# Differential attention: the first batch of a unit's transposes is copied out by ScalarE, in front of its exponentials

## The chip, the core and the metric

The kernel runs on one core of a Trainium2 chip. Its engines are TensorE (PE in the profile, PEld for its weight loads), VectorE (DVE), ScalarE (ACT), GpSimd (POOL) and SyncE (SP, which issues DMAs). Each works through its own list of instructions in order, and waits on semaphores for the others. The time is that of the device from start to end of one execution, in microseconds (us).

## The reference

A trunk of two layers on 2048 tokens of width 1024. Each layer projects the tokens once, runs three groups of attention heads on the result (latent, differential, windowed), gates and concatenates them, projects the result and normalises. The change is in the differential group: 4 heads, each with two softmax maps of which the second is subtracted, scaled by a learned factor.

```python
def block(args):                       # one block of 128 queries
    qb, bi = args
    ...
    sc = jnp.einsum('bqhmd,bkhmd->bmhqk', qb, k).astype(jnp.float32) * scale + bias[None, None]
    p = jax.nn.softmax(sc, axis=-1)
    a = p[:, 0] - lam * p[:, 1]
    return jnp.einsum('bhqk,bkhd->bqhd', a.astype(v.dtype), v)
```

## The kernel before

A layer runs in five stages: input projection, latent attention, differential attention, window attention, output projection. Between stages all engines meet at a barrier.

The function `diff_attention` works in *units*. A unit `n` is one head and one block of 128 queries, so there are 64 in a layer (4 heads of 16 blocks). Per unit there are four *score pairs*, `scores(n, m, half)`: map `m` (0 or 1) and half of the 2048 keys, each two matmuls of 128x512 into two PSUM banks. Where the band of the position bias (the block of keys at the query block and its neighbours) falls into that half, further matmuls (line 1480) add it: in the lower half of the keys for the first blocks of a head, in the upper half for the last. Three such pairs of banks form a ring, so score pair `i` of the count over all units waits until the exponential of pair `i - 3` is done.

The steps of a unit, by engine:

- TensorE: `scores` (lines 1474, 1480), `turns(n, c)` (line 1492), which transposes a quarter of the mixed probabilities, four 128x128 blocks, into the one bank TURN, and `products` (line 1507), which multiplies the transposed probabilities of two units with the values.
- VectorE: `maximum` (line 1613) of each score pair, `to_shift` (line 1620), which makes the exponential's bias of the two maxima of a map, `ratios` (lines 1629 to 1636), copies out of TURN (line 1647) and `output` (line 1656).
- ScalarE: `exp` (line 1545), two exponentials of 128x1024 for a map, `scale` (line 1552) for a quarter of the second map, copies out of TURN (line 1562) and `odd_half` (line 1570), once in two units.
- GpSimd: the rest of the mixing of the two maps, `p0 + ratio * p1`: lines 1593, 1597, 1599 and 1602. Line 1593 waits for the ratio, and line 1597 for ScalarE's `scale`.

There is one bank TURN. Batch `c` of the transposes can be made only when the copy of the batch before it is done. All copies count up the semaphore `copied`, whichever engine makes them; TensorE and the copiers take the batches in the same order.

The work is skewed by hand. Each of the three engines has one loop over `n`, and the order of the calls in its body is the order of its instructions. In round `n` the scores are those of unit `n`, and the transposes are those of unit `n - LAG` with `LAG = 2`, the last batch (and on VectorE the third) one round later. TensorE's round is: scores(n, 0, 0), batch 3 of unit n-3, scores(n, 0, 1), products, batch 0 of unit n-2, scores(n, 1, 0), batch 1, scores(n, 1, 1), products, batch 2. Batches 0 and 2 were copied by VectorE, batches 1 and 3 by ScalarE.

Of the kernel before, what the change touches and what calls it, by code (L numbers as in the profile page):

```python
# [1367 lines left out]
def diff_attention(shared, layer, carry, split_d, v_d, band_d, side_d, block_d, o_d, totals):  # L1368
# [10 lines left out]
    LAG = 2  # L1379
# [4 lines left out]
    with ctx:  # L1384
# [24 lines left out]
        def banks(n, m, half):  # L1409
            slot = (4 * n + 2 * m + half) % SLOTS  # L1410
            return psum[:, 2 * slot:2 * slot + 2, :]

        with nc.Block() as block:
# [115 lines left out]
            def copy_args(n, c):  # L1529
                dst = turned[:, n // 2 % 2, 4 * c:4 * c + 4, n % 2 * P:(n % 2 + 1) * P]  # L1530
                return dst, psum[:, TURN, :].rearrange("p (k n) -> p k n", n=P)

            @block.scalar
            def _(act):
                def exp(n, m):
                    act.wait_ge(shifted, 2 * n + m + 1)
                    if m == 0 and n >= DEEP:
                        act.wait_ge(turn_done, 4 * (n - DEEP + 1))
                    if m == 1 and n >= DEEP1:
                        act.wait_ge(mixed, 2 * (n - DEEP1 + 1))  # L1540
                    dst = probs[:, n % DEEP, :] if m == 0 else probs1[:, n % DEEP1, :]
                    if m == 0 and n >= 2:
                        act.wait_ge(summed, n - 1)
                    for half in range(2):
                        nc.scalar.activation(dst[:, half * HALF:(half + 1) * HALF].rearrange("p (a n) -> p a n", n=CH),  # L1545
                                             banks(n, m, half), ACT.Exp, bias=shift[:, n % 2, m:m + 1], scale=DIFF_SCALE,
                                             accum_out=row_sum[:, n % 2, m, half:half + 1]).then_inc(exped, 1)

                def scale(n):
                    act.wait_ge(ratio_ready, n + 1)  # L1550
                    first = probs1[:, n % DEEP1, 0:CH]
                    nc.scalar.activation(first, first, ACT.Copy, scale=ratio[:, n % 2:n % 2 + 1]).then_inc(act_scaled, 1)  # L1552

                def copy(n, c):
                    if not 0 <= n < UNITS:
                        return
                    act.wait_ge(turn_done, 4 * n + c + 1)
                    if n >= 4:

                        act.wait_ge(pv_done, n // 2 - 1)  # L1560
                    dst, src = copy_args(n, c)
                    nc.scalar.activation(dst, src, ACT.Copy).then_inc(copied, 1)

                def odd_half(g):
                    if not 0 <= g < GROUPS:
                        return
                    act.wait_ge(pv_done, g + 1)
                    if g >= 2:
                        act.wait_ge(o_ready, g - 1)
                    nc.scalar.activation(odd[:, g % 2, :], psum[DV:P, PV, 0:2 * P], ACT.Copy).then_inc(odd_out, 1)  # L1570

                act.wait_ge(dots_ready, 1)
                nc.scalar.activation(dots[:, 2:4], dots[:, 0:2], ACT.Exp).then_inc(dots_exp, 1)
                for n in range(UNITS + DRAIN + 2):
                    on = n < UNITS
                    copy(n - LAG - 1, 3)
                    if on:
                        exp(n, 0)
                    copy(n - LAG, 1)
                    if 1 <= n <= UNITS:  # L1580
                        scale(n - 1)
                    if n % 2:
                        odd_half((n - 5) // 2)
                    if on:
                        exp(n, 1)
# [24 lines left out]
            def _(dve):  # L1610
                def maximum(n, m, half):
                    dve.wait_ge(scored, 4 * n + 2 * m + half + 1)
                    nc.vector.tensor_reduce(row_max[:, n % 2, m, half:half + 1], banks(n, m, half), AX.XY, ALU.max  # L1613
                                            ).then_inc(maxed, 1)

                def to_shift(n, m):
                    dve.wait_ge(maxed, 4 * n + 2 * m + 2)
                    if n >= 2:
                        dve.wait_ge(exped, 4 * (n - 2) + 2 * m + 2)
                    nc.vector.tensor_scalar(shift[:, n % 2, m:m + 1], row_max[:, n % 2, m, 0:1],  # L1620
                                            row_max[:, n % 2, m, 1:2], -DIFF_SCALE, ALU.max, ALU.mult
                                            ).then_inc(shifted, 1)

                def ratios(n):
                    if not 0 <= n < UNITS:
                        return
                    h, qb = n // NB, n % NB
                    dve.wait_ge(exped, 4 * (n + 1))
                    nc.vector.tensor_reduce(totals[:, :, qb, h], row_sum[:, n % 2, :, :], AX.X, ALU.add
                                            ).then_inc(summed, 1)  # L1630
                    dve.wait_ge(summed, n + 1)
                    nc.vector.reciprocal(inv1[:, n % 2:n % 2 + 1], totals[:, 1, qb, h:h + 1]).then_inc(inverted, 1)
                    dve.wait_ge(inverted, n + 1)
                    if n >= 2:
                        dve.wait_ge(times_ratio, 2 * (n - 1))
                    nc.vector.tensor_scalar(ratio[:, n % 2:n % 2 + 1], inv1[:, n % 2:n % 2 + 1],
                                            totals[:, 0, qb, h:h + 1], dots[:, 0:1], ALU.mult, ALU.mult
                                            ).then_inc(ratio_ready, 1)

                def copy(n, c):  # L1640
                    if not 0 <= n < UNITS:
                        return
                    dve.wait_ge(turn_done, 4 * n + c + 1)
                    if n >= 4:
                        dve.wait_ge(pv_done, n // 2 - 1)
                    dst, src = copy_args(n, c)
                    nc.vector.tensor_copy(dst, src).then_inc(copied, 1)  # L1647

                def output(g):
                    if not 0 <= g < GROUPS:  # L1650
                        return
                    h, at = g // (NB // 2), g % (NB // 2) * 2 * P
                    dve.wait_ge(odd_out, g + 1)
                    if at == 0 and h >= 2:
                        dve.wait_ge(o_stored[h % 2], 16 * (h // 2))
                    nc.vector.tensor_tensor(o_head[:, h % 2, at:at + 2 * P], psum[0:DV, PV, 0:2 * P],
                                            odd[:, g % 2, :], ALU.add).then_inc(o_ready, 1)
# [13 lines left out]
                for n in range(UNITS + DRAIN + 2):  # L1671
                    on = n < UNITS
                    copy(n - LAG - 1, 2)
                    if on:
                        maximum(n, 0, 0)
                        maximum(n, 0, 1)
                        to_shift(n, 0)
                    copy(n - LAG, 0)
                    ratios(n - 1)
                    if on:  # L1680
                        maximum(n, 1, 0)
                        maximum(n, 1, 1)
                        to_shift(n, 1)
                    if n % 2:
                        output((n - 5) // 2)
# [720 lines left out]
```

## Time and profile before

Three runs took 4088.45 us (median), 4081.88 and 4089.66. The profiled execution took 4092.34 us, its span from the first to the last instruction 4090.5 us, at a mean granted TensorE clock of 0.977 of full speed.

| engine | busy us | share of the span |
|---|---|---|
| PE | 3788.4 | 93% |
| PEld | 2626.4 | 64% |
| POOL | 2488.2 | 61% |
| DVE | 2234.5 | 55% |
| ACT | 1657.8 | 41% |

The shares are means over stages that differ. The differential attention runs from about 1176 to 1700 us and from about 3216 to 3742 us of the span. In the table a busy share is time in which the engine executes; in rows of the timeline the first number is the start in us from the span's start, the second the duration, and in brackets stands how long the engine had been idle before, with whom it waited for.

### The profile page before, as it was taken

What the parts mean: (1) busy time and instruction counts of PE and PEld (TensorE: products, weight loads), DVE (VectorE), ACT (ScalarE), POOL (GpSimd) and SP (SyncE); (2) the same over time, 40 slices, a digit from 0 to 9 for tenths busy, and PEclk for the clock granted to TensorE, in tenths of its full rate; (3) what the DMA queues carried; (4) which work ended last, traced back from release to release, by engine and by line L of the source; (5) the groups of instructions that cost most, each with busy time, mean ns of one, the idle gap of its engine ahead of it and who ended that gap; (6) DMA issues with size and microseconds to landing.
All of it is one profiled execution on the core that took longest, in us unless ns stands there. A gap on an engine that the chain in (4) does not pass through costs nothing. (4 is left out here: it accounts for less than half of the span.)

```text
span 4090.5 us, 51527 instructions
## 1 busy us (share of the span) xinstructions
PE 3788.4 (93%) x19002; PEld 2626.4 (64%) x19002; DVE 2234.5 (55%) x3991; ACT 1657.8 (41%) x2882; POOL 2488.2 (61%) x1393
## 2 busy tenths in 40 slices
PE   8999999999989899789889999999999898997898
PEld 8788774555546565558787897755555465655587
DVE  3012135555569999675430021255555699996754
ACT  3112104333358888661031121033333588886610
POOL 1221326877769999755512213277777699997555
PEclk9999999999989999999989999999999899999999
DMA  5333534342220222325353335323322202223353
GB/s 178 124 138 117 169 115 109 78 101 64 57 56 1 56 56 52 91 83 184 130 177 124 129 120 152 130 57 75 75 65 57 56 1 56 56 52 90 88 181 129
DMA packets 179680, 391.38 MB, mean 96 GB/s; under 512 B 17854, under 2 KB 98984, under 8 KB 167784
## 3 DMA queue, kind: packets, MB, share of 16 engines
q1 hardware_dynamic: 178568, 386.70, 33.9%
q8 instruction: 152, 2.49, 0.3%
q10 hardware_dynamic: 864, 1.41, 0.2%
q14 instruction: 96, 0.79, 0.1%
HBM read 254.88 MB, written 135.67 MB: 95 GB/s over the span
## 5 line engine op out<-in xcount | busy, mean ns | idle before, releaser
L1279 POOL TENSOR_TENSOR mla_sum_pool<-mla_sum_pool,mla_probs 128x1024 f32<-128x1024 f32 (+1 forms) x336 | 777.9, 2315 | 207.0 <-ACT mla_probs L1240 182.2
L1297 DVE TENSOR_REDUCE carry_row_max<-psum 128x1 f32<-128x512 f32 x688 | 474.4, 690 | 413.6 <-PE psum L1112 409.1
L1240 ACT ACTIVATE mla_probs<-psum 128x1024 f32<-128x1024 f32 x384 | 373.3, 1021 | 693.6 <-PE psum L1149 686.4
L1545 ACT ACTIVATE diff_probs<-psum,diff_shift 128x1024 f32<-128x1024 f32 x512 | 566.1, 1111 | 195.3 <-DVE diff_shift L1620 189.7
L1613 DVE TENSOR_REDUCE diff_row_max<-psum 128x1 f32<-128x1024 f32 x512 | 612.5, 1218 | 52.5 <-PE psum L1480 38.3
L1492 PE MATMUL psum<-ident,diff_probs 128*128 128x128 f32 x2048 | 329.8, 284 | 107.1 <-DVE diff_turned L1647 72.6
L624 PE MATMUL psum<-in_x_hi,in_w_hi 128*128 128x512 f32 x1024 | 404.5, 395 | 2.7 <-ACT in_mla_val L733 2.7
L624 PE MATMUL psum<-carry_firsts,in_w_hi 128*128 128x512 f32 x1024 | 404.8, 395 | 0.0
L624 PE MATMUL psum<-in_x_hi,in_w_lo 128*128 128x512 f32 x1024 | 401.6, 392 | 0.0
L1492 PEld LDWEIGHTS psum<-ident,diff_probs 128*128 128x128 f32 x2048 | 215.8, 141 | 285.5 <-issue 188.5
L1162 PE MATMUL psum<-mla_probs,mla_v_op 128*64 128x512 f32 x1536 | 373.1, 607 | 0.0
L1597 POOL TENSOR_TENSOR diff_probs<-diff_probs 128x1024 f32<-128x1024 f32 x128 | 304.0, 2375 | 22.5 <-ACT diff_probs L1552 4.6
L1602 POOL TENSOR_TENSOR diff_probs<-diff_probs 128x1024 f32<-128x1024 f32 x128 | 304.0, 2375 | 10.0
L519 POOL CAST in_w_hi<-in_w_raw 128x1024 fp32r<-128x1024 f32 x64 | 66.6, 1040 | 360.3 <-PE psum L624 360.3
L580 PE MATMUL psum<-carry_weights,in_x_hi 128*128 128x384 f32 x1024 | 269.6, 345 | 14.4 <-DVE carry_weights L860 14.4
L1134 PE MATMUL psum<-carry_weights 128*128 128x512 f32 x768 | 256.2, 415 | 5.3 <-PEq L115 3.6
L1599 POOL TENSOR_TENSOR diff_probs<-diff_probs,diff_ratio 128x1024 f32<-128x1024 f32 x128 | 242.7, 1896 | 0.0
L624 PEld LDWEIGHTS psum<-in_x_hi,in_w_hi 128*128 128x128 f32 x1024 | 194.6, 190 | 47.1 <-issue 4.1
L624 PEld LDWEIGHTS psum<-in_x_hi,in_w_lo 128*128 128x128 f32 x1024 | 194.2, 190 | 43.6
L624 PEld LDWEIGHTS psum<-carry_firsts,in_w_hi 128*128 128x128 f32 x1024 | 194.3, 190 | 41.7
L935 DVE TENSOR_TENSOR in_out<-psum,in_out 128x1024 fp32r<-128x1024 f32 x32 | 39.1, 1221 | 332.8 <-ACT in_out L819 332.7
L1474 PE MATMUL psum<-carry_firsts 128*128 128x512 f32 x512 | 190.8, 457 | 27.5 <-PEq L115 17.0
(206 smaller groups left out, 7369.1 us busy)
## 6 DMA issues: line engine op xcount, KB each, us to landing
in_w_raw<-in_w_in SPq DMA_DIRECT2D x64, 512.0 KB, 3.9
split_d<-in_out SPq DMA_DIRECT2D x64, 512.0 KB, 2.6
raw_d<-in_out SPq DMA_DIRECT2D x32, 512.0 KB, 2.6
mq_d<-in_out SPq DMA_DIRECT2D x48, 256.0 KB, 3.4
mk_d<-in_out SPq DMA_DIRECT2D x48, 256.0 KB, 3.8
carry_firsts<-split_d SPq DMA_DIRECT2D x48, 256.0 KB, 7.9
carry_weights<-split_d SPq DMA_DIRECT2D x48, 256.0 KB, 7.7
carry_weights<-split_d SPq DMA_DIRECT2D x16, 768.0 KB, 17.7
```

The source lines that it names most:

```text
L580: last = nc.tensor.matmul(psum[:, bank, 0:GROUP], xt[:, k, at], w[:, k, :], start=(k == 0 and n == 0), stop=(k == KD - 1 and n == 2))
L624: last = nc.tensor.matmul(psum[:, tile_slot(g) + ch, :], w[:, s, k, :], xt[:, k, ch * CH:(ch + 1) * CH], start=(k == 0 and n == 0), stop=( ...
L1134: nc.tensor.matmul(psum[:, S0 + 2 * (s % 2) + a, :], k_[b][:, keys], q_[b][:, at], start=(m == 0), stop=False)
L1162: last = nc.tensor.matmul(psum[a * DV:(a + 1) * DV, PV, :], v_op[:, b, kb, :], probs[:, s % RING, a * CH:(a + 1) * CH], start=(kb == 0), s ...
L1240: nc.scalar.activation(probs[:, s % RING, :].rearrange("p (a n) -> p a n", n=CH), psum[:, S0 + 2 * (s % 2):S0 + 2 * (s % 2) + 2, :], ACT.E ...
L1279: nc.gpsimd.tensor_tensor(acc, start, probs[:, s % RING, mine], ALU.add).then_inc(pool_added, 1)
L1297: nc.vector.tensor_reduce(row_max[:, u % 2, qb, n:n + 1], psum[:, sweep_bank(g), :], AX.X, ALU.max).then_inc(maxed, 1)
L1492: last = nc.tensor.transpose(psum[:, TURN, k * P:(k + 1) * P], probs[:, n % DEEP, kb * P:(kb + 1) * P], ident[:, :])
L1545: nc.scalar.activation(dst[:, half * HALF:(half + 1) * HALF].rearrange("p (a n) -> p a n", n=CH), banks(n, m, half), ACT.Exp, bias=shift[: ...
L1597: nc.gpsimd.tensor_tensor(probs[:, n % DEEP, 0:HALF], probs[:, n % DEEP, 0:HALF], probs1[:, n % DEEP1, 0:HALF], ALU.add).then_inc(mixed, 1)
L1602: nc.gpsimd.tensor_tensor(probs[:, n % DEEP, HALF:SEQ], probs[:, n % DEEP, HALF:SEQ], third, ALU.add).then_inc(mixed, 1)
L1613: nc.vector.tensor_reduce(row_max[:, n % 2, m, half:half + 1], banks(n, m, half), AX.XY, ALU.max).then_inc(maxed, 1)
```

## The change

In ScalarE's round the copy of batch 0 of unit `n - LAG` is put in front of `exp(n, 0)`, and in VectorE's round it is taken out from between `to_shift(n, 0)` and `ratios(n - 1)`. ScalarE then copies batches 3, 0 and 1, VectorE batch 2. Line numbers behind the first edit grow by one.

```diff
@@ -1574,6 +1574,7 @@
                 for n in range(UNITS + DRAIN + 2):
                     on = n < UNITS
                     copy(n - LAG - 1, 3)
+                    copy(n - LAG, 0)
                     if on:
                         exp(n, 0)
                     copy(n - LAG, 1)
@@ -1675,7 +1676,6 @@
                         maximum(n, 0, 0)
                         maximum(n, 0, 1)
                         to_shift(n, 0)
-                    copy(n - LAG, 0)
                     ratios(n - 1)
                     if on:
                         maximum(n, 1, 0)
```

ScalarE before, around the fifth odd half of the first layer's stage (`diff_probs<-psum,diff_shift` is an exponential, `diff_turned<-psum` a copy out of TURN, `diff_probs<-diff_probs,diff_ratio` the scaling):

```order
L1545 ACTIVATE diff_probs,diff_row_sum<-psum,diff_shift 128x1024 x2
L1562 ACTIVATE diff_turned<-psum 128x4x128
L1545 ACTIVATE diff_probs,diff_row_sum<-psum,diff_shift 128x1024 x2
L1562 ACTIVATE diff_turned<-psum 128x4x128
L1552 ACTIVATE diff_probs<-diff_probs,diff_ratio 128x512
L1570 ACTIVATE diff_odd<-psum 64x256
L1545 ACTIVATE diff_probs,diff_row_sum<-psum,diff_shift 128x1024 x2
L1562 ACTIVATE diff_turned<-psum 128x4x128
L1545 ACTIVATE diff_probs,diff_row_sum<-psum,diff_shift 128x1024 x2
```

ScalarE in the changed kernel, the same place:

```order
L1545 ACTIVATE diff_probs,diff_row_sum<-psum,diff_shift 128x1024 x2
L1562 ACTIVATE diff_turned<-psum 128x4x128 x2
L1545 ACTIVATE diff_probs,diff_row_sum<-psum,diff_shift 128x1024 x2
L1562 ACTIVATE diff_turned<-psum 128x4x128
L1552 ACTIVATE diff_probs<-diff_probs,diff_ratio 128x512
L1570 ACTIVATE diff_odd<-psum 64x256
L1545 ACTIVATE diff_probs,diff_row_sum<-psum,diff_shift 128x1024 x2
L1562 ACTIVATE diff_turned<-psum 128x4x128 x2
L1545 ACTIVATE diff_probs,diff_row_sum<-psum,diff_shift 128x1024 x2
```

The copy behind the second map's exponentials, which was one, is now two in a row: batch 3 of the older unit and batch 0 of the next, both ahead of the next round's first exponential.

VectorE before, around the fourth output of the first layer's stage (`diff_o_head`; `diff_shift` is a map's shift, `diff_turned` a copy out of TURN):

```order
L1620 TENSOR_SCALAR diff_shift<-diff_row_max 128x1
L1647 COPY diff_turned<-psum 128x4x128
L1629 TENSOR_REDUCE totals<-diff_row_sum 128x2
L1632 RECIPROCAL diff_inv<-totals 128x1
L1636 TENSOR_SCALAR diff_ratio<-diff_inv,totals,diff_dots 128x1
L1613 TENSOR_REDUCE diff_row_max<-psum 128x1 x2
L1620 TENSOR_SCALAR diff_shift<-diff_row_max 128x1
L1656 TENSOR_TENSOR diff_o_head<-psum,diff_odd 64x256
L1647 COPY diff_turned<-psum 128x4x128
L1613 TENSOR_REDUCE diff_row_max<-psum 128x1 x2
L1620 TENSOR_SCALAR diff_shift<-diff_row_max 128x1
```

VectorE in the changed kernel, the same place:

```order
L1621 TENSOR_SCALAR diff_shift<-diff_row_max 128x1
L1630 TENSOR_REDUCE totals<-diff_row_sum 128x2
L1633 RECIPROCAL diff_inv<-totals 128x1
L1637 TENSOR_SCALAR diff_ratio<-diff_inv,totals,diff_dots 128x1
L1614 TENSOR_REDUCE diff_row_max<-psum 128x1 x2
L1621 TENSOR_SCALAR diff_shift<-diff_row_max 128x1
L1657 TENSOR_TENSOR diff_o_head<-psum,diff_odd 64x256
L1648 COPY diff_turned<-psum 128x4x128
L1614 TENSOR_REDUCE diff_row_max<-psum 128x1 x2
L1621 TENSOR_SCALAR diff_shift<-diff_row_max 128x1
```

The copy between the shift of the first map (L1620, now L1621) and the sums and ratio (L1629 to L1636, now L1630 to L1637) is gone. TensorE's and GpSimd's instructions are the same in number and order.

## Rows read from the trace of the kernel before

**Rows 1.** Busy time by engine in a steady stretch of the first differential-attention stage.
```profile
core 0: us, PE busy (x) PEld busy (x) DVE busy (x) ACT busy (x) POOL busy (x), PEclk, DMA share, GB/s
1205.20:1682.90 477.70, 430.60 (x2764) 284.55 (x2764) 429.66 (x697) 387.04 (x698) 463.83 (x246) 1.00 0.16 36
```

**Rows 2.** Timeline of POOL alone: first operation of the third, second-last and last unit.
```profile
start us, us, engine line op out<-in xcount [idle before <-releaser]
1205.23 1.04 POOL L1593 TENSOR_TENSOR diff_probs<-diff_probs,diff_ratio 128x512 f32<-128x512 f32 x1
...
1675.08 1.04 POOL L1593 TENSOR_TENSOR diff_probs<-diff_probs,diff_ratio 128x512 f32<-128x512 f32 x1
...
1682.85 1.04 POOL L1593 TENSOR_TENSOR diff_probs<-diff_probs,diff_ratio 128x512 f32<-128x512 f32 x1
```

**Rows 3.** Timeline of all engines, unit 41 of 64, first layer (query block 9).
```profile
1499.41 1.12 ACT L1545 ACTIVATE diff_probs<-psum,diff_shift 128x1024 f32<-128x1024 f32 x1 [1.24 <-DVE diff_shift L1620]
...
1500.50 0.27 DVE L1636 TENSOR_SCALAR diff_ratio<-diff_inv,totals,diff_dots 128x1 f32<-128x1 f32 x1
...
1500.73 0.71 PE L1474 MATMUL psum<-carry_firsts 128*128 128x512 f32 x2
...
1501.61 0.59 ACT L1562 ACTIVATE diff_turned<-psum 128x512 f32<-128x512 f32 x1
...
1501.72 1.08 PE L1507 MATMUL psum<-diff_turned,carry_rows 128*64 128x256 f32 x8
1502.08 0.73 ACT L1552 ACTIVATE diff_probs<-diff_probs,diff_ratio 128x512 f32<-128x512 f32 x1
1502.63 1.06 POOL L1593 TENSOR_TENSOR diff_probs<-diff_probs,diff_ratio 128x512 f32<-128x512 f32 x1
...
1502.74 0.66 PE L1492 MATMUL psum<-ident,diff_probs 128*128 128x128 f32 x4
1502.85 0.38 ACT L1570 ACTIVATE diff_odd<-psum 64x256 f32<-64x256 f32 x1
...
1503.26 0.42 DVE L1656 TENSOR_TENSOR diff_o_head<-psum,diff_odd 64x256 f32<-64x256 f32 x1
...
1503.61 0.67 DVE L1647 COPY diff_turned<-psum 128x512 f32<-128x512 f32 x1
1503.83 2.38 POOL L1597 TENSOR_TENSOR diff_probs<-diff_probs 128x1024 f32<-128x1024 f32 x1
...
1504.42 0.63 PE L1492 MATMUL psum<-ident,diff_probs 128*128 128x128 f32 x4 [0.56 <-DVE diff_turned L1647]
...
1504.81 0.71 PE L1474 MATMUL psum<-carry_firsts 128*128 128x512 f32 x2
...
1505.91 1.23 DVE L1613 TENSOR_REDUCE diff_row_max<-psum 128x1 f32<-128x1024 f32 x1 [0.50 <-PE psum L1480]
...
1506.82 0.66 PE L1492 MATMUL psum<-ident,diff_probs 128*128 128x128 f32 x4
1507.17 0.21 DVE L1620 TENSOR_SCALAR diff_shift<-diff_row_max 128x1 f32<-128x1 f32 x1
...
1507.42 1.11 ACT L1545 ACTIVATE diff_probs<-psum,diff_shift 128x1024 f32<-128x1024 f32 x1 [1.30 <-DVE diff_shift L1620]
1507.51 0.69 DVE L1647 COPY diff_turned<-psum 128x512 f32<-128x512 f32 x1
...
1508.35 0.63 PE L1492 MATMUL psum<-ident,diff_probs 128*128 128x128 f32 x4 [0.41 <-DVE diff_turned L1647]
```

**Rows 4.** Timeline of all engines, units 15 to 17, band in the lower half.
```profile
1302.06 0.71 PE L1474 MATMUL psum<-carry_weights 128*128 128x512 f32 x2
...
1302.70 1.08 PE L1507 MATMUL psum<-diff_turned,carry_rows 128*64 128x256 f32 x8
...
1304.32 1.12 ACT L1545 ACTIVATE diff_probs<-psum,diff_shift 128x1024 f32<-128x1024 f32 x1 [0.95 <-DVE diff_shift L1620]
...
1308.22 1.11 ACT L1545 ACTIVATE diff_probs<-psum,diff_shift 128x1024 f32<-128x1024 f32 x1 [0.51 <-DVE diff_shift L1620]
...
1309.47 0.30 PEld L1474 LDWEIGHTS psum<-carry_weights 128*128 128x128 f32 x2 [0.16 <-ACT diff_probs L1545]
...
1311.75 1.12 ACT L1545 ACTIVATE diff_probs<-psum,diff_shift 128x1024 f32<-128x1024 f32 x1 [0.75 <-DVE diff_shift L1620]
```

## The prediction

> **What bounds the kernel now.** I read the page's strip of 40 slices first, to find the two stretches that the change touches, one differential-attention stage in each layer; then the busy times of a steady stretch of one; then the timeline of GpSimd alone; then the timeline of all engines over one unit. All times are of the one profiled execution: span 4090.5 us, 4092.3 us in all, 3.9 us above the median of the three runs.
>
> In the steady stretch GpSimd is busy 463.83 of 477.70 us, 97%, TensorE and VectorE 90%, ScalarE 81% [rows 1]. From the third unit to the last, the first of GpSimd's four operations (L1593) starts 61 times later than at 1205.23, at 1682.85: 7.83 us a unit, back to back [rows 2]. So GpSimd sets the pace, and VectorE, from which the change takes work, does not.
>
> The other engines make a loop of their own, which I call the front. Its period is from the first exponential of a unit to that of the next. In rows 3 (unit 41, the tenth query block of its head; exponential at 1499.41, next at 1507.42) it took 8.01 us; in the first half of a head, where the band of the bias lies in the lower half of the keys, 7.43 us (1304.32 to 1311.75) [rows 4]. The front is slower than GpSimd in one half of a head and catches up in the other. It can, because what GpSimd takes from it comes early: the ratio is ready at 1500.50 + 0.27 = 1500.77, and L1593 starts at 1502.63; ScalarE's scaling ends at 1502.08 + 0.73 = 1502.81, and L1597, which needs it, starts at 1503.83 [rows 3]. That is 1.9 and 1.0 us of slack.
>
> **The change part by part.** TensorE's order is unchanged. Each unit loses one 128x512 copy on VectorE (0.69, next instruction 0.60 later) and gains one on ScalarE (0.59, next instruction 0.47 later: 1501.61 to 1502.08) [rows 3]. By busy time both fit: ScalarE goes from 387.04/61 = 6.3 to 6.8 us a unit, under 7.83 [rows 1]. The question is the place.
>
> The copy now stands in front of both exponentials of the first map. It waits for the first batch of transposes of the unit two earlier, which TensorE issues behind this unit's second score pair and four product matmuls. In rows 3 these transposes start at 1506.82 and are done by 1507.51, when VectorE's copy starts; the shift for which the exponential waited was ready at 1507.38, and the exponential started at 1507.42. With the copy in front it can start at 1507.51 + 0.47 = 1507.98 at best: 0.56 us later. Queued behind the waiting copy are both exponentials, the copy of batch 1, the scaling that GpSimd's L1597 needs, and the second map's exponentials.
>
> The exponential also frees the PSUM slot for the fourth score pair of the unit (three slots in a ring). So there is a new loop. Its links, each a start-to-start time, for a unit with the band in the upper half:
> - exponential to fourth score pair: 1.25 (1308.22 to 1309.47, the one row where this wait shows [rows 4]);
> - score pair to products: 0.99 (1500.73 to 1501.72);
> - products to batch 2 of transposes: 1.02 (1501.72 to 1502.74);
> - batch 2, its copy on VectorE, batch 3: 0.69 + 0.84 = 1.53 (1506.82 to 1507.51 to 1508.35, the same sequence with VectorE free);
> - batch 3 to second score pair: 0.39 (1504.42 to 1504.81);
> - score pair to products to batch 0: 0.99 + 1.02 (1504.81 to 1506.82);
> - batch 0 to its copy 0.69, copy to exponential 0.47.
>
> Sum 8.35 us [rows 3, 4]. In every second unit there is more. VectorE adds the output before it copies batch 2, and that needs ScalarE's odd half, which now stands behind two exponentials (1.11 each), the copy 0.47 and the scaling 0.77 (1502.08 to 1502.85): 3.45 us after the exponential. From there 0.41 to the output (1502.85 to 1503.26), 0.35 to the copy (to 1503.61) and 0.84 to batch 3: batch 3 at 5.05 instead of 4.79, so 8.61. Mean of the upper half of a head: 8.48.
>
> With the band in the lower half the two score pairs of the loop have no band matmuls and take 0.64 instead of 0.99 (1302.06 to 1302.70 [rows 4]). The even unit is 8.35 - 0.70 = 7.65. The odd one gains only the second pair's 0.35, since its output chain starts at the exponential: 8.61 - 0.35 = 8.26. Mean 7.96.
>
> The front then averages (8.48 + 7.96)/2 = 8.22 us over the 16 units of a head, against GpSimd's 7.83. It no longer catches up, and the slack of 1.0 us is used up once a layer. The excess is 0.39 x 16 = 6.2 us a head, 50 us for the eight heads of both layers, less 2 x 1.0 for the slack and less the first two and the last two units of each layer, where the copy doesn't stand before an exponential or GpSimd alone sets the end (about 2 us): 46 us. I take 46. What could lie under it: the 0.77 after the scaling may itself be a wait for the products (they end at 1502.80); with the scaling's own length less the 0.1 by which ScalarE's instructions overlap, 0.63, the odd units lose 0.14 each, 0.07 x 128 = 9 us less. What could lie above it: every link stretched by a wait of 0.05 us on TensorE, 0.2 a unit, 26 us more.
>
> What VectorE saves doesn't shorten the front's loop. VectorE already stands idle 0.50 before a maximum when the scores come late (1505.91 [rows 3]), and the copy it keeps (batch 2) waits for transposes in both kernels. Ends of the stage: the last products come after GpSimd's last addition, with batches 2 and 3 copied by the same engines as before. I cost both at nothing.
>
> The Trainium skill (Perfetto Trace Analysis, Optimizing Scalar/DVE Operations) says that moving work to ScalarE may make sense where VectorE is saturated. VectorE at 90% looks it [rows 1], and were it the bound, the 0.60 it sheds would be worth up to 77 us. The trace disagrees with the premise: GpSimd's starts are 7.83 us apart without a gap [rows 2].
>
> **The rivals.**
> (1) *GpSimd still sets the pace.* The copy's delay of 0.56 us a unit is less than the slack of 1.0 us. If the front's new loop comes out under 7.83 on average over a head (the copy starting sooner than the old start of VectorE's), nothing moves: 4088 us. For it: the slack is real. Against: the links above are all measured, and 0.39 us a unit is much to lose.
> (2) *Faster: GpSimd's own operations get shorter when VectorE copies less.* Near the end of a stage, where VectorE has little left to do, L1593 starts 7.77 us apart (1675.08 to 1682.85) against 7.83 [rows 2]. All of this in every unit would be 0.06 x 126 = 8 us, 4081. It decides only if the front stays under 7.8, and it is worth under 0.2%; with twice that price 4073.
> The Trainium skill (SBUF — State Buffer, Who interferes with whom) speaks against this rival: a VectorE instruction with at most one SBUF input, outside its two-port modes, does not contend with GpSimd, and this copy reads PSUM. By that rule the gain is nothing; no row here separates this copy's effect from VectorE's others.
> (3) *Every unit pays the whole delay.* If the front had no room in either half, the copy would add its 0.56 to the 8.01 and more, and all units would run near the odd upper ones, 8.4 to 8.5 us: 0.62 x 126 = 78 us, 4166. For it: TensorE is then idle for the exponential in every unit, and its granted clock, 1.00 in this stretch [rows 1], could fall. Against: the lower-half units have 0.4 us of room now.
>
> **How the numbers follow.** On the footing of the median: 4088.5 + 46 = 4134 us. Chances: the new loop, 0.66 (its own range 4112 to 4152); rival 3, 0.16; rival 1, 0.12; rival 2, 0.06. What a measurement of this kernel can tell from no change is about 0.2%, 8 us. Slower by more than that takes the forecast and rival 3, and a small part of rival 1 (an excess of some tenths of a microsecond in the upper halves alone): 0.84. Within 0.2%: 0.11. Faster: 0.05. The range of 8 in 10 goes from 4095, just over the edge of no change, to 4166, rival 3.
>
> **What would show it right or wrong.** Right: GpSimd's L1593 starts 8.1 to 8.3 us apart on average, near 8.5 in the second half of a head and 7.9 in the first; a new wait of L1597 for ScalarE's scaling, some 45 us in both layers; TensorE's score matmuls wait for ScalarE's exponential in nearly every unit; ScalarE's exponential no longer waits for the shift but the copy before it waits for transposes; GpSimd's busy time unchanged near 2488 us. Wrong: GpSimd's starts still 7.83 apart (rival 1), operations of GpSimd shorter (rival 2), or 8.4 and over in both halves or a granted clock below 1.00 in the stage (rival 3). A shift of time outside the two stages would be none of these.

## The result and the profile after

The changed kernel took 4133.52 us (median of four, 4129.33 to 4137.62), the kernel before 4089.05 us in the same comparison: a ratio of 1.011, interval 1.0096 to 1.0124, or 39 to 51 us more. The forecast was 4134. One run of a later variant (e6), 6479.70 us at a mean granted clock of 0.706, is a slow outlier and is left out of every figure below.

Busy time by engine in a stretch that answers to [rows 1], from the start of the third unit to that of the second-last:

```profile
core 0: us, PE busy (x) PEld busy (x) DVE busy (x) ACT busy (x) POOL busy (x), PEclk, DMA share, GB/s
1205.23:1698.40 493.17, 436.53 (x2723) 282.59 (x2724) 394.74 (x629) 410.52 (x748) 455.35 (x241) 1.00 0.16 35
```

VectorE's share fell from 90% to 80% (394.74 of 493.17), ScalarE's rose from 81% to 83%, and GpSimd, at 97% before, is at 92%. The granted clock is 1.00 in both. TensorE fell from 90% to 89%. No engine is full any more, and the stage is longer: a sign of a loop of waits. GpSimd's busy time in the whole execution is 2485.8 us, 2.4 less than before.

GpSimd's first operation, alone, for units 2, 32, 39, 48 and 63 of the first layer (answers to [rows 2]; the line is now L1594):

```profile
start us, us, engine line op out<-in xcount [idle before <-releaser]
1205.11 1.04 POOL L1594 TENSOR_TENSOR diff_probs<-diff_probs,diff_ratio 128x512 f32<-128x512 f32 x1
...
1451.79 1.04 POOL L1594 TENSOR_TENSOR diff_probs<-diff_probs,diff_ratio 128x512 f32<-128x512 f32 x1
...
1507.35 1.04 POOL L1594 TENSOR_TENSOR diff_probs<-diff_probs,diff_ratio 128x512 f32<-128x512 f32 x1
...
1583.33 1.03 POOL L1594 TENSOR_TENSOR diff_probs<-diff_probs,diff_ratio 128x512 f32<-128x512 f32 x1
...
1706.63 1.04 POOL L1594 TENSOR_TENSOR diff_probs<-diff_probs,diff_ratio 128x512 f32<-128x512 f32 x1
```

From the third unit to the last, (1706.63 - 1205.11)/61 = 8.22 us a unit instead of 7.83. Units 32 to 39 take 7.94 each, units 39 to 48 take 8.44. The single steps in the first half of a head are 7.82 and 8.08 by turns, in the second 8.24 to 8.71.

Who waited for whom in the steady stretch, in all, times and longest (some of the rows):

```profile
engine line waited for: us in total, times, longest us
...
ACT diff_turned L1562 <- PE psum L1492: 70.4, 60, 1.5
...
PEld psum L1474 <- ACT diff_probs L1545: 36.7, 60, 0.6
POOL diff_probs L1598 <- ACT diff_probs L1552: 31.1, 46, 1.1
...
PE psum L1474 <- ACT diff_probs L1545: 22.4, 60, 0.4
...
ACT diff_probs L1545 <- DVE diff_shift L1621: 7.8, 16, 0.6
```

Three of these waits are new or have grown from almost nothing. ScalarE's copy waits for the transposes, 70.4 us, where in the kernel before the exponential waited for the shift (84.1 us in 93 waits; 7.8 us in 16 are left). GpSimd's L1598 waits 31.1 us for ScalarE's scaling; before, that wait was 0.2 us, once. TensorE's score matmuls wait for the exponential 60 times, once a unit; before, only their weight loads did, 4 times, 0.6 us in all.

One even unit and the start of the odd one behind it, in the second half of a head (answers to [rows 3]; the columns are the same):

```profile
1522.51 1.11 ACT L1545 ACTIVATE diff_probs<-psum,diff_shift 128x1024 f32<-128x1024 f32 x1
...
1523.76 0.73 PE L1474 MATMUL psum<-carry_firsts 128*128 128x512 f32 x2 [0.38 <-ACT diff_probs L1545]
...
1524.78 1.08 PE L1507 MATMUL psum<-diff_turned,carry_rows 128*64 128x256 f32 x8
...
1525.79 0.66 PE L1492 MATMUL psum<-ident,diff_probs 128*128 128x128 f32 x4
1525.98 2.37 POOL L1598 TENSOR_TENSOR diff_probs<-diff_probs 128x1024 f32<-128x1024 f32 x1 [0.92 <-ACT diff_probs L1552]
...
1526.48 0.69 DVE L1648 COPY diff_turned<-psum 128x512 f32<-128x512 f32 x1
...
1527.32 0.63 PE L1492 MATMUL psum<-ident,diff_probs 128*128 128x128 f32 x4 [0.41 <-DVE diff_turned L1648]
...
1527.70 0.71 PE L1474 MATMUL psum<-carry_firsts 128*128 128x512 f32 x2
1528.25 0.58 PE L1480 MATMUL psum<-carry_ups,ident_r 128*128 128x256 f32 x4
...
1528.76 1.08 PE L1507 MATMUL psum<-diff_turned,carry_rows 128*64 128x256 f32 x8
...
1529.78 0.66 PE L1492 MATMUL psum<-ident,diff_probs 128*128 128x128 f32 x4
1530.13 0.21 DVE L1621 TENSOR_SCALAR diff_shift<-diff_row_max 128x1 f32<-128x1 f32 x1
...
1530.47 0.60 ACT L1562 ACTIVATE diff_turned<-psum 128x512 f32<-128x512 f32 x1 [1.29 <-PE psum L1492]
...
1530.96 1.11 ACT L1545 ACTIVATE diff_probs<-psum,diff_shift 128x1024 f32<-128x1024 f32 x1
...
1534.41 0.38 ACT L1570 ACTIVATE diff_odd<-psum 64x256 f32<-64x256 f32 x1
...
1535.99 0.63 PE L1492 MATMUL psum<-ident,diff_probs 128*128 128x128 f32 x4 [0.57 <-DVE diff_turned L1648]
```

The reader can follow the loop down the list: the exponential at 1522.51, the score pair that it holds up at 1523.76, products 1524.78, batch 2 1525.79, VectorE's copy 1526.48, batch 3 1527.32, score pair 1527.70, products 1528.76, batch 0 1529.78, ScalarE's copy 1530.47 and the exponential at 1530.96. Between neighbours of this list lies the work of the first (for a score pair with its band matmuls, L1480) and a hand-over, nothing else. The shift was ready at 1530.13 + 0.21 = 1530.34, 0.62 before its exponential.

### The profile page after: what moved, and what is told of

The parts are those of the page before. It is cut to its first block and busy times, and to the rows that moved or that the text cites. A ratio compares the mean times of both kernels' runs of the same rounds, so it can differ in the third digit from the quotient of the medians.

```text
span 4127.3 us, 51527 instructions
## 1 busy us (share of the span) xinstructions
PE 3802.3 (92%) x19002; PEld 2620.3 (63%) x19002; DVE 2168.2 (53%) x3863; ACT 1720.9 (42%) x3010; POOL 2485.8 (60%) x1393
## 5 line engine op out<-in xcount | busy, mean ns | idle before, releaser
L1614 DVE TENSOR_REDUCE diff_row_max<-psum 128x1 f32<-128x1024 f32 x512 | 623.4, 1222 | 177.1 <-PE psum L1480 140.1
L1598 POOL TENSOR_TENSOR diff_probs<-diff_probs 128x1024 f32<-128x1024 f32 x128 | 303.8, 2373 | 72.2 <-ACT diff_probs L1552 67.9
L1562 ACT ACTIVATE diff_turned<-psum 128x512 f32<-128x512 f32 x384 | 229.8, 598 | 162.7 <-PE psum L1492 162.7
```

The lines of the kernel that those rows point to most:

```text
L1598: nc.gpsimd.tensor_tensor(probs[:, n % DEEP, 0:HALF], probs[:, n % DEEP, 0:HALF], probs1[:, n % DEEP1, 0:HALF], ALU.add).then_inc(mixed, 1)
```

## The experiments

All ratios are to the kernel before, in runs on the same chip. "A step" is the time between two starts of GpSimd's first operation, one unit apart. Units 32 to 39 stand for the first half of a head, 39 to 48 for the second.

**Is it ScalarE's load?** (e1)

```diff
 ScalarE, kernel before, in each round:
                     copy(n - LAG - 1, 3)
+                    for b in range(2):      # units 0 to 63
+                        nc.scalar.activation(idle[:, b, :], ident[:, :], ACT.Copy)
                     if on:
                         exp(n, 0)
```

`idle` is a new tile that nothing reads; a semaphore, long since counted up, keeps a round's copies behind the last round's.

> The kernel before with extra work on ScalarE alone: two 128x128 copies of a constant in front of each first exponential, waiting for nothing; all four batches are copied as before. Theory A (the loss is the copy's wait for batch 0 of the transposes plus its own time, in front of the exponentials, which makes a new loop): ScalarE stands idle about 1.3 us before that exponential in the kernel before, the extra 0.5 us disappears in it: 4089 us, within 6. Rival B (the loss is ScalarE's load): as the change, 4125 to 4135. Rival C (the loss comes with VectorE's missing copy, or with who empties the transposes' bank): 4089.

Measured 4093.38 us, ratio 1.001 (0.9998 to 1.0021). ScalarE's timeline:

```profile
1498.99 0.51 ACT L1572 ACTIVATE diff_idle<-ident 128x128 bf16<-128x128 f32 x2
1500.31 1.12 ACT L1547 ACTIVATE diff_probs<-psum,diff_shift 128x1024 f32<-128x1024 f32 x1 [0.81 <-DVE diff_shift L1631]
```

The two small copies lie in the idle time, the exponential still waits 0.81 for the shift, and the steps are 7.83, as before. The load is free; rival B falls.

**Is it who makes the copy?** (e2) The same, with one line in front of the two small copies:

```diff
+                    act.wait_ge(turn_done, 4 * (n - LAG) + 1)
```

> As e1_extra_no_wait, but the extra work on ScalarE waits for batch 0 of the transposes, as the moved copy does; VectorE still makes the copy itself. Theory A: the whole loss is back although no copy was moved: 4134 us, 4125 to 4142; GpSimd's first operation starts in the same uneven steps, about 8.5 us in the second half of a head and 7.8 and 8.1 by turns in the first. Rival B: as e1_extra_no_wait. Rival C: 4089.

Measured 4129.22 us, ratio 1.0097 (1.0077 to 1.0117). ScalarE's extra work, the exponential and the score pair behind it:

```profile
1498.74 0.51 ACT L1573 ACTIVATE diff_idle<-ident 128x128 bf16<-128x128 f32 x2 [1.05 <-PE psum L1494]
...
1499.16 1.10 ACT L1547 ACTIVATE diff_probs<-psum,diff_shift 128x1024 f32<-128x1024 f32 x1
...
1500.40 0.72 PE L1476 MATMUL psum<-carry_firsts 128*128 128x512 f32 x2 [0.19 <-ACT diff_probs L1547]
```

VectorE still makes all its copies, and almost the whole loss is there; steps 8.35 in units 39 to 48 and 7.86 in 32 to 39, 8.13 on average. The expectation had 8.5, and 7.8 and 8.1 by turns. The extra work holds the exponential back by 0.42 us (1498.74 to 1499.16), where the moved copy takes 0.47 to 0.49, which is the direction of the difference to 8.22. VectorE makes one copy a unit more here than in the changed kernel, and the loss is no larger for it. This copies the mechanism without moving the work. Rival C falls.

**Is it the wait alone?** (e3)

```diff
 ScalarE, kernel before, in exp(n, 0):
                         act.wait_ge(summed, n - 1)
+                        act.wait_ge(turn_done, 4 * (n - LAG) + 1)
```

> The kernel before, where the first exponential waits for batch 0 of the transposes, with no work in between. Theory A: the transposes are done 0.1 us after the old start of the exponential (1507.51 against 1507.42), the loop is then 8.35 - 0.47 = 7.88 in the upper half of a head and 7.2 in the lower, still 7.83 or under on average: 4089 to 4098 us. Rival D (the wait by itself is what costs, whatever comes behind it): 4125 to 4135. Rival B: 4089.

Measured 4097.93 us, ratio 1.0023 (1.0013 to 1.0033): 9 us, at the upper end of what theory A gave and far from rival D. The steps are 7.82 in the first half of a head and 7.94 in the second, where three of the nine reach 8.06 to 8.23. So the 44 us are the wait and the copy's own 0.48 together; about a fifth of it is there with the wait alone.

**Is the place the price?** (e5)

```diff
 ScalarE, changed kernel:
-                    copy(n - LAG, 0)
                     if on:
                         exp(n, 0)
+                    copy(n - LAG, 0)
                     copy(n - LAG, 1)
```

> The changed kernel with ScalarE's new copy of batch 0 behind the two exponentials of the first map instead of in front of them. The instructions on each engine are the same in number. Theory A, whose price is the place in the loop: batch 1 on TensorE now waits for both exponentials and the copy (2.2 + 0.59 + 0.14), so the fourth score pair comes 3.3 us after the exponential instead of 1.25; the loop is 3.3 + 0.99 + 1.02 + 1.53 + 0.39 + 1.10 + 1.26 + 0.25 = 9.8 us in the upper half and 9.1 in the lower, 1.6 to 1.7 us over 7.83 in each of 126 units: about 4300 us, 4270 to 4320. Rivals B and C (the load, or who copies): as the change, 4134.

Measured 4403.37 us (two runs), ratio 1.0766 (1.0727 to 1.0805). The direction is right, the size isn't: 2.5 us a unit where 1.7 were expected. The copy and batch 1, then TensorE in two neighbouring units, then two stretches by engine:

```profile
1505.25 0.59 ACT L1562 ACTIVATE diff_turned<-psum 128x512 f32<-128x512 f32 x1
...
1505.98 0.63 PE L1492 MATMUL psum<-ident,diff_probs 128*128 128x128 f32 x4 [2.41 <-ACT diff_turned L1562]
```

```profile
1265.94 0.71 PE L1474 MATMUL psum<-carry_firsts 128*128 128x512 f32 x2
...
1273.72 1.20 PE L1474 MATMUL psum<-carry_firsts 128*128 128x512 f32 x2
```

```profile
core 0: us, PE busy (x) PEld busy (x) DVE busy (x) ACT busy (x) POOL busy (x), PEclk, DMA share, GB/s
1255.00:1305.00 50.00, 35.78 (x225) 24.05 (x222) 32.21 (x53) 33.87 (x61) 37.20 (x20) 0.96 0.00 1
1305.00:1355.00 50.00, 39.35 (x215) 24.82 (x214) 31.06 (x47) 32.12 (x57) 35.50 (x19) 0.86 0.00 1
```

TensorE waits 2.41 for the copy at 1505.98, as expected. But the granted clock is 0.86 and 0.96 in these two stretches and 0.92 over the stage of the first layer, and a pair of score matmuls that takes 0.71 at 1265.94 takes 1.20 at 1273.72. From 1274 to 1276 us the granted clock reads 0.50. The shortest steps, 9.14, are the forecast 9.1 of the lower half; the others are up to 11.6, and the mean is 10.34. By an estimate, 0.08 of the stage's 630.8 us, 50 us or 0.8 us a unit, is the most that the lower clock can have cost there; that is about the size of the miss, but no run takes it apart from the waits.

**The output's place in the odd units** (e4)

```diff
 VectorE, changed kernel:
                     copy(n - LAG - 1, 2)
+                    if n % 2 == 0:
+                        output((n - 6) // 2)
                     if on:
                         maximum(n, 0, 0)
...
-                    if n % 2:
-                        output((n - 5) // 2)
```

> The changed kernel, where VectorE adds the output of two units behind its copy of batch 2 instead of in front of it. Theory A has a term for this order: in every second unit batch 3 waits for the output, which waits for ScalarE's odd half behind the moved copy. In the changed kernel's trace the second half of a head alternates by about 0.2 us around the even units and the first half steps 7.82, 8.08. Without the term all units go by the even chain: upper half down 0.1 us on average, lower half at 7.82 or just over: 8 x 0.1 + 4 x 0.2 = 1.6 us a head less, 13 us in both layers: 4120 us, 4114 to 4126. Rival E (that term is not on the path; only the delay of the copy is): no change from the changed kernel, 4133.

Measured 4124.86 us, ratio 1.0091 (1.0078 to 1.0104), against 1.011. The steps of units 32 to 39 fall to 7.82, those of 39 to 48 to 8.33, on average 8.12 instead of 8.22; 0.10 x 126 is 13 us by the trace, 8 by the two ratios. The term is real. Its size by time alone is not settled, as the intervals of the two ratios overlap; the steps settle it, whose means over a half of a head agree within 0.01 us between the two layers.

**One half of a head (e6, e13), and every second unit (e7)**

```diff
 changed kernel, ScalarE and VectorE:
-                    copy(n - LAG, 0)                         # ScalarE
+                    if n % NB < NB // 2:
+                        copy(n - LAG, 0)
...
+                    if not (n % NB < NB // 2):                # VectorE, behind to_shift(n, 0)
+                        copy(n - LAG, 0)
```

> The moved copy on ScalarE only in rounds where the scores are of the first eight blocks of a head; in the other eight VectorE copies as before. Theory A: the steps of the first half stay as in the changed kernel (7.82 and 8.08 by turns), those of the second half are the old 7.82 with at most some 0.2 in a few units: 4 x 0.26 to 0.3 a head plus 0.5 to 1 us, 8 heads: 12 to 20 us over before, 4104 us (4098 to 4110). A rival by which each moved copy costs the same (44 us over 128 units) gives half the loss: 4111.

Measured 4106.39 us (median of three), ratio 1.0044 (1.0029 to 1.0059): 18 us, with an interval of 12 to 24. That holds the theory's loss as well as the rival's, so the time doesn't tell them apart; the steps do:

> The kernel of e6_lower_half_only again, for its profile. Theory A: GpSimd's first operation steps 7.82 and 8.08 by turns in the first half of each head and 7.82 to about 8.1 in a few units of the second. A rival by which each moved copy costs the same: all units of the first half at 8.2, all of the second at 7.82.

One run, 4102.31 us beside 4084.99 of the kernel before. GpSimd's first operation of units 32, 39 and 48:

```profile
start us, us, engine line op out<-in xcount [idle before <-releaser]
1446.61 1.05 POOL L1595 TENSOR_TENSOR diff_probs<-diff_probs,diff_ratio 128x512 f32<-128x512 f32 x1
...
1502.21 1.05 POOL L1595 TENSOR_TENSOR diff_probs<-diff_probs,diff_ratio 128x512 f32<-128x512 f32 x1
...
1573.82 1.04 POOL L1595 TENSOR_TENSOR diff_probs<-diff_probs,diff_ratio 128x512 f32<-128x512 f32 x1
```

Units 32 to 39 take 7.94, by turns 7.82 and 8.10, as in the changed kernel. But units 39 to 48 take 7.96, and the steps into units 40 to 47, in whose rounds all copies are made as before, take 7.93 on average (7.80 to 8.18). I had expected this in a few units; it is most of them. In the kernel before, the front is slower than GpSimd in the second half of a head and lives on what it gained in the first. Its trace shows it. This is ScalarE's scaling and the GpSimd operation that needs it, in unit 36 and in unit 45:

```profile
1470.43 0.72 ACT L1552 ACTIVATE diff_probs<-diff_probs,diff_ratio 128x512 f32<-128x512 f32 x1
...
1472.50 2.39 POOL L1597 TENSOR_TENSOR diff_probs<-diff_probs 128x1024 f32<-128x1024 f32 x1
...
1542.11 0.73 ACT L1552 ACTIVATE diff_probs<-diff_probs,diff_ratio 128x512 f32<-128x512 f32 x1
...
1542.96 2.38 POOL L1597 TENSOR_TENSOR diff_probs<-diff_probs 128x1024 f32<-128x1024 f32 x1
```

In unit 36 the scaled values lie ready for 1.35 us, in unit 45 for 0.12. Take away the gain of the first half and the second half pays too.

With the condition `n % 2 == 0` in the same two places (e7):

> The changed kernel with the copy moved to ScalarE only in even units, those without an output behind them; VectorE copies batch 0 in the odd ones. Theory A: the first half of a head is all 7.82 (the even units' loop was under it and the odd ones' term is gone), the second half alternates between 7.8 and 8.6: 4107 us (4100 to 4113). A rival by which each moved copy costs the same gives half of 44: 4110; the steps tell them apart, since by it both halves of a head would lose.

Measured 4108.53 us, ratio 1.0042 (1.0028 to 1.0056). Units 32 to 39 take 7.81, units 39 to 48 8.09, going to and fro between 7.82 and 8.77. The first half loses nothing, as the theory has it; a fixed price for each copy would have shown there.

**TensorE's order** (e12)

```diff
 TensorE, changed kernel:
-                    products(n, 0)
                     turns(n - LAG, 0)
+                    products(n, 0)
```

> The changed kernel, where TensorE makes batch 0 of the transposes in front of the four product matmuls instead of behind them. Theory A: the 1.02 of the products leaves the way from the second score pair to the copy, so the exponential waits for the shift again; the loop through the copy shrinks from 8.35 to about 7.4. But batch 0 then needs GpSimd's L1598 of that unit 1 us earlier, and that waits for the scaling behind the exponentials: a new loop through GpSimd of about 8.0 us (L1598 2.37, transposes and copy 0.7 + 0.5, the exponentials 2.2, the copy 0.5, the scaling 0.7, hand-overs). Steps of 8.0 to 8.1 in both halves, no longer apart by the place of the band: 4112 us (4100 to 4122). Rival (all of the loss is the products' 1.02 in the path): 4088. Rival (nothing gained): 4133.

Measured 4128.71 us, ratio 1.0091 (1.0075 to 1.0106): the time missed, 16 us above the expectation. The steps are 8.27 in the first half of a head and 8.06 in the second, so the band's place no longer makes the second half the slower one; 8.0 to 8.1 was expected in both. Three rows show the new link:

```profile
1503.09 0.59 ACT L1562 ACTIVATE diff_turned<-psum 128x512 f32<-128x512 f32 x1
...
1503.82 0.63 PE L1492 MATMUL psum<-ident,diff_probs 128*128 128x128 f32 x4 [0.77 <-ACT diff_turned L1562]
...
1504.49 0.60 ACT L1562 ACTIVATE diff_turned<-psum 128x512 f32<-128x512 f32 x1 [0.81 <-PE psum L1492]
```

Batch 0 now comes so early that it waits 0.77 for ScalarE's copy of batch 3, which stands behind the second map's exponentials. Transposes wait for a copy of ScalarE 61 times in the steady stretch of the first layer, 40.2 us in all. The wait of the transposes for GpSimd's L1598 that I had named shows only 5 times, 5.9 us.

**Moving both loops.** If two loops near 7.8 us hold each other, an edit to either brings nothing and both together bring something. On the kernel before: the later output of above (e10), ScalarE scaling 640 columns and GpSimd 384 (e9), and both (e8).

```diff
-                    first = probs1[:, n % DEEP1, 0:CH]                       # ScalarE
+                    first = probs1[:, n % DEEP1, 0:CH + 128]
...
-                    second, third = probs1[:, n % DEEP1, CH:HALF], ...       # GpSimd
+                    second, third = probs1[:, n % DEEP1, CH + 128:HALF], ...
```

> The kernel before with VectorE's output behind the copy of batch 2, nothing else. Theory A: GpSimd sets the pace, so a faster front brings nothing: 4088 us, down 0 to 3. Rival (the front sets part of the pace in the kernel before): down 10 or more.

> Only the second half of e8_before_output_later_more_scaling: ScalarE scales 640 columns, GpSimd 384, and VectorE's output stays in front of the copy of batch 2. Theory A: GpSimd's loop falls to 7.61, but the front with the output in the old place is near 7.6 to 7.7 in the first half and 7.8 to 8.1 in the second: between 0 and 8 us less than before, 4084 us, so that the two edits together bring more than the sum of each. Rival (e8's gain is all from GpSimd's shorter operation): as e8, 4076.

> The kernel before with the output later as in e10_before_output_later, and ScalarE scales 640 columns of the second map instead of 512, GpSimd 384 instead of 512 in its first operation. GpSimd saves 128/512 of 1.04 less its fixed part, about 0.24 us a unit, ScalarE gains 0.13. Theory A: both loops are moved at once; GpSimd's 7.59, the front 7.8 to 7.9 in the upper half and 7.5 in the lower, so 7.6 to 7.7 on average: 14 to 20 us less than before, 4072 us (4066 to 4080). Rival (GpSimd alone sets the pace, the front has room to spare): 0.24 x 126 = 30 us less, 4058. Rival (no gain, since ScalarE's longer scaling delays the second map's exponentials): 4088.

| kernel | ratio to before | interval | mean step, units 2 to 63 |
|---|---|---|---|
| output later (e10) | 0.9998 | 0.9989 to 1.0007 | 7.83 |
| more scaling on ScalarE (e9) | 0.9988 | 0.9979 to 0.9997 | 7.79 |
| both (e8) | 0.9970 | 0.9959 to 0.9981 | 7.70 |

GpSimd's first operation in the kernel with both, units 32, 39 and 48:

```profile
start us, us, engine line op out<-in xcount [idle before <-releaser]
1445.09 0.83 POOL L1593 TENSOR_TENSOR diff_probs<-diff_probs,diff_ratio 128x384 f32<-128x384 f32 x1
...
1498.37 0.82 POOL L1593 TENSOR_TENSOR diff_probs<-diff_probs,diff_ratio 128x384 f32<-128x384 f32 x1
...
1568.18 0.83 POOL L1593 TENSOR_TENSOR diff_probs<-diff_probs,diff_ratio 128x384 f32<-128x384 f32 x1
```

In the first half of a head GpSimd sets the pace, at its new 7.61; in the second the front does, 7.76. Alone, the shorter operation gave 7.61 and 7.93. The kernel with both edits, at 4076.01 us the fastest of the study, beats both kernels of the case. Its gain of 12 us (8 to 17) lies at the lower edge of the 14 to 20 that I expected. By time alone it isn't settled that the two edits together bring more than their sum, as the intervals are about 4 us wide to either side; by the steps it is: 0.13 us a unit together, against 0.04 and at most 0.01 alone.

## Why the prediction was right

- *GpSimd bounds the kernel before, with a front just under it.* Right; e10 brought nothing (0.9998), and e9 and e8 show the second limit. The slack of 1.0 us was a reading of one unit, though: it goes from 1.35 to 0.12 within a head (shown with e13).
- *The copy in front makes a new loop of 8.35 us.* Measured in the unit above: 8.45 (1522.51 to 1530.96). The links: 1.25 for 1.25, score pair 1.02 for 0.99, 1.01 for 1.02, 0.69 + 0.84 as forecast, 0.38 for 0.39, then 1.06 + 1.02 for 0.99 + 1.02, and 0.69 + 0.49 for 0.69 + 0.47. The link that grew is a score pair whose band falls into two banks: four band matmuls instead of two (1528.25).
- *The odd unit's term.* The odd half was forecast 3.45 us after the exponential and batch 3 5.05: measured 1534.41 - 1530.96 = 3.45 and 1535.99 - 1530.96 = 5.03. e4 takes the term away: 0.10 us a unit.
- *Halves of a head.* Forecast 8.48 and 7.96 with eight units each; measured 8.44 over nine and 7.94 over seven. The mean is the forecast 8.22. That it fits so closely is partly luck: both means were a little high, and the boundary lay one unit off. The single steps differ from the forecast pairs. In the first half they are 7.82 and 8.08 instead of 7.65 and 8.26, since GpSimd itself takes 7.8, with the same sum (15.90 and 15.91). In the second they aren't two values but rise to 8.71 and fall again.
- *The sum.* Forecast 46 us. GpSimd's first to last start grew from 1187.71 to 1682.85 = 495.1 to 519.1 us in the first layer, and by 24.2 in the second: 48.1 us in the two profiled executions. Their spans differ by only 36.8. The other 11 us lie outside the stages, where the instructions are the same: the profiled execution of before was above its median, that of after the fastest of its four. By the medians the loss is 44.5.
- *The signs.* The idle time in front of GpSimd's L1598, in both layers, grew from 22.5 to 72.2 us, where a new wait of some 45 was forecast. TensorE's wait for the exponential is there in every unit, and the exponential's wait for the shift is all but gone.
- *Costed at nothing.* ScalarE's load cost nothing (e1). VectorE's relief shows no gain: e2, without it, loses no more than the changed kernel. GpSimd's operations are 2.4 us shorter in all, so rival 2 had its sign right and next to nothing of its size.
- *The granted clock.* It stayed at 1.00, so rival 3 had no ground; e5 shows a case in which it fell.
- *One reason was too simple.* The prediction charged the loss to each unit's own loop. e13 shows that part of a second half's loss comes from the first half, which no longer builds up a lead. The sum was right all the same, since it compared averages over a head.

The Trainium skill's rule on relieving a saturated VectorE (Perfetto Trace Analysis, Optimizing Scalar/DVE Operations) didn't help here, as its condition was not met: VectorE was 90% busy and not the bound.

## What to carry to other kernels

Before moving work from one engine to another, walk once around the loop from an instruction to the same instruction one round later, link by link with start-to-start times, and compare it with the period of the busiest engine. An engine's idle time in front of an instruction can take extra work, as long as this work waits for nothing later than that instruction did. Where two loops are nearly equal, shorten both in one edit before judging either.

## What the runs showed of the hardware

With TensorE 72 to 79% busy and waits of 2.2 us on average for ScalarE's copy, once a unit, its granted clock was 0.96 and 0.86 in two stretches of 50 us (e5): parts of them ran at the lower of the two levels, 1.2 instead of 2.4 GHz, and a pair of score matmuls took 1.20 instead of 0.71 there. With TensorE 89% busy and no wait of its matmuls over 0.9 us in the steady stretch (the changed kernel) it stayed at 1.00. So a loop of waits on TensorE's path can cost more than its links add up to: in e5 the mean step is 10.34 us, where the links gave 9.1 and 9.8.
